# Pooling's neighbour sums moved behind the convolution, and one of two weightings of V moved from VectorE to GpSimd

## The reference

```python
def _pool_mixer(u, w_pool_l, s_pool_l):          # windows 2, 4, 8, 16 over neighbouring tokens
    csum = cumulative sum of u over tokens
    for g, w in enumerate(POOL_WINDOWS):
        mean = (cs[:, hi] - cs[:, lo]) / (hi - lo)
        parts.append(mean - uf[group g])
    y = einsum('btgc,gce->btge', stack(parts), w_pool_l)
    return y * s_pool_l

def _conformer_conv(u, ...):                     # 31 taps, depthwise
    a, g = split(u); h = a * sigmoid(g)
    h = depthwise_conv(h, conv_w_l) + conv_b_l
    return silu(layer_norm(h)) @ w_pw2_l

def _ret_scan(kc, vc, s0):                       # retention, chunks of 128 tokens
    kv = einsum('bhncd,hc,bhnce->nbhde', kc, w_end, vc)
    scan: s -> chunk_decay * s + kv_n            # once forward, once backward
```

## Time and profile before

| | |
|---|---|
| median of 3 runs | 3274.9 us (3274.47 to 3276.96) |
| profiled execution, time | 3276.12 us |
| profiled execution, span from first to last instruction | 3274.0 us |
| PE busy | 2883.8 us, 88% |
| DVE busy | 1996.9 us, 61% |
| ACT busy | 1204.8 us, 37% |
| POOL busy | 608.8 us, 19% |
| mean granted clock of PE | 0.944 of full speed |

### The profile page before, as it was taken

The page is one execution under the profiler, slowest core; times in us unless marked ns, Lnnn a source line. Parts: engine busy times, 40 slices in busy tenths (PEclk is TensorE's granted clock), DMA queues, the critical chain, the costliest instruction groups (busy, mean ns, idle before and its releaser), DMA issues.

```text
span 3274.0 us, 46686 instructions
## 1 busy us (share of the span) xinstructions
PE 2883.8 (88%) x17578; PEld 1603.1 (49%) x17578; DVE 1996.9 (61%) x2744; ACT 1204.8 (37%) x2076; POOL 608.8 (19%) x456
## 2 busy tenths in 40 slices
PE   4799896878999999999997579896789899999997
PEld 3455562554545656757754234463554344444443
DVE  5894687884366414636645695578883664274765
ACT  5111325775444212313324311326773443231332
POOL 0500021000225302202212230011001243120311
PEclk8899996999999999999998789998999999999998
DMA  5111111221134321111141221212222242112133
GB/s 207 55 40 38 36 43 42 89 82 58 60 124 135 121 77 46 49 42 44 48 147 34 96 71 39 49 41 81 101 101 71 93 139 83 45 52 64 52 130 115
DMA packets 69312, 248.90 MB, mean 76 GB/s; under 512 B 9248, under 2 KB 10016, under 8 KB 69152
## 3 DMA queue, kind: packets, MB, share of 16 engines
q1 hardware_dynamic: 68000, 241.44, 22.0%
q10 hardware_dynamic: 1152, 5.24, 0.4%
HBM read 221.75 MB, written 19.92 MB: 74 GB/s over the span
## 4 chain that ended last, share of the span: by engine, by line
PE 61%; issue 18%; DVE 12%; ACT 5%; POOL 2%; DMA 1%; SPq 0%; DVEq 0%; POOLq 0%; ACTq 0%
PE PS L777 36%; PE PS L882 17%; DVE R L2139 4%; DVE wlo L1801 2%; PE PS L1178 2%; ACT X L1430 1%; ACT R L1428 1%; DVE R L1963 1%; DVE R L1950 1%; ACT whi L1313 1%; POOL R L2541 1%; DMA R<-in_w_ada 1%; PE PS L1102 1%; PE PS L1201 1%; PE PS L811 1%
## 5 line engine op out<-in xcount | busy, mean ns | idle before, releaser
L777 PE MATMUL PS<-R,whi 128*128 128x512 f16 (+1 forms) x5216 | 1428.6, 361 | 98.8 <-DVE wlo L1801 57.4
L777 PE MATMUL PS<-R,wlo 128*128 128x512 f16 (+1 forms) x2608 | 940.5, 361 | 0.0
L777 PEld LDWEIGHTS PS<-R,whi 128*128 128x128 f16 x5216 | 509.5, 99 | 633.6 <-issue 72.5
L882 PE MATMUL PS<-R,whi 128*128 128x256 f16 (+2 forms) x2352 | 510.3, 326 | 0.0
L1801 DVE SCALAR_TENSOR_TENSOR wlo<-stage,whi 128x1024 f16<-128x1024 f32 (+1 forms) x204 | 278.6, 1366 | 364.6 <-ACT whi L1313 363.7
L777 PEld LDWEIGHTS PS<-R,wlo 128*128 128x128 f16 x2608 | 257.9, 99 | 256.6 <-issue 14.9
L882 PE MATMUL PS<-R,wlo 128*128 128x256 f16 (+2 forms) x1176 | 319.1, 326 | 0.0
L882 PEld LDWEIGHTS PS<-R,whi 128*128 128x128 f16 x2352 | 230.1, 98 | 152.0
L1313 ACT ACTIVATE whi<-stage 128x1024 f16<-128x1024 f32 (+1 forms) x204 | 210.4, 1031 | 140.4 <-PE PS L777 85.0
L2139 DVE SCALAR_TENSOR_TENSOR R<-X,small,R 128x1024 f32<-128x1024 f32 (+1 forms) x180 | 218.9, 1263 | 1.8
L2468 POOL TENSOR_TENSOR X<-X 128x512 f32<-128x512 f32 (+1 forms) x98 | 135.5, 1386 | 453.7 <-ACT X L1705 331.9
(11 more groups left out here) (219 smaller groups left out, 3468.8 us busy)
## 6 DMA issues: line engine op xcount, KB each, us to landing
stage<-in_w_gu SPq DMA_DIRECT2D x120, 512.0 KB, 3.8
X<-in_w_ada SPq DMA_DIRECT2D x60, 512.0 KB, 3.3
stage<-in_w_down SPq DMA_DIRECT2D x48, 512.0 KB, 3.4
stage<-in_w_in SPq DMA_DIRECT2D x44, 512.0 KB, 3.3
stage<-in_w_out SPq DMA_DIRECT2D x32, 512.0 KB, 3.3
h_save<-R SPq DMA_DIRECT2D x24, 640.0 KB, 5.3
R<-h_save SPq DMA_DIRECT2D x24, 640.0 KB, 4.6
T<-in_w_ada SPq DMA_DIRECT2D x20, 512.0 KB, 3.6
```

What stands on the lines that cost most here:

```text
L777: last = mm(slot(into, t0, t1)[:, c0 - t0:c1 - t0], w[:, j, k, :], row, start=(k == 0 and q == 0), stop=(k == K - 1 and q == 2))
L882: last = mm(s_bank(nf, t, o, n), w[:, j, k0 + k, :], row, start=(k == 0 and x == 0), stop=(k == PAIRS - 1 and x == 2))
```

## The change

Three things change. The pooling sums are started by POOL only when the last tap of the convolution is done (`conv`), and their padded rows and their table lie in the rows `H` in place of `G` and `Y`; so ACT no longer waits for `pooled` ahead of unit 6, but ahead of reading out unit 16, which is written to row `H`. To have the rows `H` free in layer 1, SP saves them to HBM right as the last step of layer 0 finishes each of them, and the tables `cnt` are loaded only behind `u_done` and `h_saved`, in front of the rotary tables. Of the two weightings of V, the forward one goes to POOL, which counts `vw_fwd`.

```diff
-        Gpad = R[:, G:G + 7, :] ... 6 padded rows
+        Gpad = R[:, G:G + 3, :] ... 2 padded rows
+        Hpad = R[:, H:H + 5, :] ... 4 padded rows
...
@@ SP
                 else:
-                    sp.wait_ge(S["h_rows"], rows_before(4 * l + 1, 0))
+                    sp.wait_ge(S["h_back"], 16 * KD * 2 * l)
+                    for d in range(KD):
+                        sp.wait_ge(S["h_rows"], rows_before(4 * l - 1, 1) + d + 1)
+                        sp.dma_start(h_save[d], R[:, H + d, :]).then_inc(S["h_saved"], 16)
                     sp.wait_ge(S["stk_ps"], ...)
-                for j in range(2):
-                    sp.dma_start(R[:, Y + j, :], a["cnt"][j]).then_inc(S["cd_tab"], 16)
                 sp.dma_start(SW[:, :], a["swb"][l]).then_inc(S["cd_tab"], 16)
                 sp.dma_start(perm[:, :], a["permB"]).then_inc(S["cd_tab"], 16)
                 sp.wait_ge(S["u_done"], rows_before(4 * l + 2, 0))
+                if l:
+                    sp.wait_ge(S["h_saved"], 16 * KD * 2 * l)
+                for j in range(2):
+                    sp.dma_start(R[:, H + 5 + j, :], a["cnt"][j]).then_inc(S["cd_tab"], 16)
                 for j in range(2):
                     sp.dma_start(xrow(2 + j), a["ropeB"][j]).then_inc(S["b_tab"], 16)
-                (units 2 to 9, in layer 1 each followed by a save of one row H)
-                stream(unit0(l, "in") + 2 + KD, ahead - 2 - KD, KD, a["w_in"][l][2 + KD:ahead])
+                stream(unit0(l, "in") + 2, ahead - 2, KD, a["w_in"][l][2:ahead])
...
-                if l:
-                    sp.wait_ge(S["h_saved"], 16 * KD * 2 * l)
                 swap(0)
@@ PE
                     pe.wait_ge(S["vw"], at("vw", l) + i + 1)
+                    pe.wait_ge(S["vw_fwd"], at("vw_fwd", l) + i + 1)
@@ ACT
+                if l:
+                    act.wait_ge(S["h_saved"], 16 * KD * 2 * l)      # ahead of unit 0's read-out
-                (units 2 and 3 to Gpad[:, 2, :] and Gpad[:, 3, :])
+                (units 2 and 3 to Hpad[:, 0, :] and Hpad[:, 1, :])
                 act.wait_ge(S["glu"], at("glu", l) + 2)
-                act.wait_ge(S["pooled"], at("pooled", l) + 2)
...
-                if l:
-                    act.wait_ge(S["h_saved"], 16 * KD * 2 * l)
+                act.wait_ge(S["pooled"], at("pooled", l) + 2)
                 a_row(16, 1)
@@ DVE
                     TT(heads(T[:, 512 + c:768 + c]), heads(vtok[:, t, :]), by_head(8, 1), ALU.mult)
-                    TT(heads(vw_fwd[:, c:c + 256]), heads(vtok[:, t, :]), by_head(8, 0), ALU.mult).then_inc(S["vw"], 1)
+                    (the first one now counts vw)
@@ POOL
                 pool.wait_ge(S["cd_tab"], at("cd_tab", l) + 64)
+                pool.wait_ge(S["conv"], at("conv", l) + TAPS * 2 * len(segs(l)))
                 for j in range(2):
                     pool.wait_ge(S["slot_free"], u0 + 3 + j)
-                    src = Gpad[:, 2 + j, :]
-                    a_, b_ = Gpad[:, 4, :], Gpad[:, 5, :]
+                    src = Hpad[:, j, :]
+                    a_, b_ = Hpad[:, 2, :], Hpad[:, 3, :]
...
                 pool.memset(Sb[:, B_ORDER[0], :], 0.0).then_inc(S["states_zero"], 1)
+                pool.wait_ge(S["pw_ps"], at("pw_ps", l) + 2 * len(spans(t0)))
+                for i in range(NTILE):
+                    pool.wait_ge(S["v_tok"], at("v_tok", l) + i + 1)
+                    if i >= 2:
+                        pool.wait_ge(S["kv_ps"], at("kv_ps", l) + i - 1)
+                    TT(heads(vw_fwd[:, (i % 2) * 256:(i % 2) * 256 + 256]), heads(vtok[:, B_ORDER[i], :]), by_head(8, 0),
+                       ALU.mult).then_inc(S["vw_fwd"], 1)
```

More of the change, by code:

```diff
@@ L196, in build @@
         Xpad = X[:, :].rearrange("p (r t) -> p r t", r=4)
-        Gpad = R[:, G:G + 7, :].rearrange("p r t -> p (r t)")[:, 0:6 * PADW].rearrange("p (r t) -> p r t", r=6)
+        Gpad = R[:, G:G + 3, :].rearrange("p r t -> p (r t)")[:, 0:2 * PADW].rearrange("p (r t) -> p r t", r=2)
+        Hpad = R[:, H:H + 5, :].rearrange("p r t -> p (r t)")[:, 0:4 * PADW].rearrange("p (r t) -> p r t", r=4)
         vtok = X[:, 0:NTILE * 256].rearrange("p (t c) -> p t c", c=256)
@@ L245, in build @@
             b_tab=32, gate_tanh=4, roped_ps=12, roped=12, d_tab=16,
-            states_zero=1, tr_ps=NTILE, v_tok=NTILE, k_tok=NTILE, vw=NTILE, kv_ps=NTILE, state=NTILE - 1, kv_fwd=NTILE - 1,
+            states_zero=1, tr_ps=NTILE, v_tok=NTILE, k_tok=NTILE, vw=NTILE, vw_fwd=NTILE, kv_ps=NTILE, state=NTILE - 1, kv_fwd=NTILE - 1,
             state_fwd=NTILE - 1,
@@ L453, in build, with by_head @@
         block = ctx.enter_context(nc.Block())
+        def by_head(col0, half):
+            return rtab[:, col0 + 4 * half:col0 + 4 * half + 4].rearrange("p (h e) -> p h e", e=1).to_broadcast([P, HB, 64])
+        heads = lambda ap: ap.rearrange("p (h e) -> p h e", h=HB)
         B_ORDER = [1, 0] + list(range(NTILE - 1, CT - 1, -1))
@@ L1555, in _ @@
                 u0 = unit0(l, "in")
-                kinds = ((ACT.Tanh, Gpad[:, 0, :]), (ACT.Copy, Xpad[:, 0, :]), (ACT.Copy, Gpad[:, 2, :]),
-                         (ACT.Copy, Gpad[:, 3, :]), (ACT.Tanh, Gpad[:, 1, :]), (ACT.Copy, Xpad[:, 1, :]))
+                if l:
+                    act.wait_ge(S["h_saved"], 16 * KD * 2 * l)
+                kinds = ((ACT.Tanh, Gpad[:, 0, :]), (ACT.Copy, Xpad[:, 0, :]), (ACT.Copy, Hpad[:, 0, :]),
+                         (ACT.Copy, Hpad[:, 1, :]), (ACT.Tanh, Gpad[:, 1, :]), (ACT.Copy, Xpad[:, 1, :]))
                 for i, (kind, dst) in enumerate(kinds):
@@ L2501, in _ @@
                     pool.wait_ge(S["slot_free"], u0)
+                    pool.wait_ge(S["h_saved"], 16 * KD * 2 * l)
                 gaps = [(0, HALF), (HALF + CTX, HALF), (PADW - HALF, HALF)] if not t0 else \
@@ L2504, in _ @@
                 for g0, n in gaps:
-                    pool.memset(Gpad[:, 2:4, g0:g0 + n], 0.0)
+                    pool.memset(Hpad[:, 0:2, g0:g0 + n], 0.0)
                     last = pool.memset(Xpad[:, 0:2, g0:g0 + n], 0.0)
@@ L2522, in _ @@
                             last = TT(R[half:half + 64, Y + 2 + j, c0:c0 + n], w[half:half + 64, p0:p0 + n],
-                                      R[half:half + 64, Y + j, c0:c0 + n], ALU.mult)
+                                      R[half:half + 64, H + 5 + j, c0:c0 + n], ALU.mult)
                     own.link(last)
```

12 lines of the change are left out of this document (1 added, 11 removed).

## The result

| | before | after |
|---|---|---|
| median of 4 runs | 3274.68 us (3273.78 to 3276.96) | 3226.66 us (3223.84 to 3231.61) |
| profiled execution, time | 3276.12 us | 3231.61 us |
| profiled execution, span | 3274.0 us | 3229.8 us |
| PE busy | 2883.8 us | 2881.9 us |
| DVE busy | 1996.9 us | 1973.3 us |

The ratio of the times is 0.9855, with a 95% interval from 0.9842 to 0.9867: 48 us faster.

The account below looks back on a forecast made before the run. PE, 88% busy, was taken as the bound. 25.0 + 20.6 + 6.2 - 3.0 - 1.1 = 47.7 us off 3276.1 gives 3228.4, put at 3227 us against the runs' median; 8 in 10 range 3218 to 3246.

Parts of the forecast that it names:

- taps, layer 0: Convolution taps no longer beside POOL's sums, so PE never stalls and unit 7 ends at 173.7 us; gain 25.0 us.
- taps, layer 1: Same in layer 1: taps at undisturbed length, units up to 7 end at 1933.9 us, before 1954.6; gain 20.6 us.
- V's weighting, both layers: Retention's state loop: DVE loses the forward product, 0.34 us for each of nine chunks; gain 3.1 us a layer, 6.2 in all.
- contention, layer 1: Moved sums lengthen DVE's instructions in the rotary units, stalling PE at units 13 and 14; cost 3.0 us, at most 10.7.
- contention, layer 0: Moved sums beside layer 0's rotary units, where a unit with its rotary products takes 14.3 us; cost 0, at most 5.
- table DMAs: Two table rows ahead of unit 2's weights: hidden in layer 0, unit 2 late in layer 1; cost 1.1 us, bounds 0 and 3.
- rival 2: State loop: POOL's product comes first, DVE waits, chunks take 2.5 us, not 1.65; 16 us, total 3243 us; chance 0.11.
- five exposed instructions: Rotary units: five DVE instructions per unit with both inputs in SBUF, slowed beside POOL's sums to 2.75 us each.
- 11.6 of PE plus what slack is left: Layer 1, unit 14: PE's time set against DVE's about 17 us, leaving a stall of 1.6 us.
- the rule: Shared ports held for each instruction's whole duration: layer 1 stall about 6 us, total 3 us higher.
- the rows gave 3.0: Layer 1 rotary units: cost from the profiled pitch of taps beside POOL's sums, 3.3 us, taken as 2.75 for rotary instructions.
- twice the costs: Contention and DMA costs doubled, given as the slow end, 3236 us, of the forecast's own range from 3219.

Follow-up runs that it names:

- experiment 3: Changed kernel without POOL's wait for the convolution's last tap, so the sums start beside the first taps as before; 3271.0 us.
- the next two profiles: Profiles of two repeat runs of the changed kernel, nothing altered; medians 3227.36 and 3227.57 us.
- experiment 4: Changed kernel with the pooling sums left out, one fill with zeros per row in their place; 3225.14 us.
- experiment 7: Changed kernel with four waits among POOL's twelve sums of layer 1, so they run where DVE is idle; 3224.51 us.
- Experiments 6 and 8: Weights of units 2 and 3 requested ahead of the table rows: on the changed kernel with lo formed earlier, 3227.9 us; on it with paced sums, 3220.3 us.
- the second run of the changed kernel: The changed kernel run again with nothing altered; median 3227.36 us, span of its profile 3226.0 us.

## Why the prediction was right, step by step

It said 3227 us; the median is 3226.7. By terms, gains positive:

| term | predicted | the stages show |
|---|---|---|
| taps, layer 0 | +25.0 | 102.93 - 77.88 = +25.05 |
| taps, layer 1 | +20.6 | 88.05 - 68.12 + 0.72 = +20.65 |
| V's weighting, both layers | +6.2 | 2 x 2.4 = +4.8 |
| contention, layer 1 | -3.0 | 1.6 + 2.4 = -4.0 |
| contention, layer 0 | 0 | 0 |
| table DMAs | -1.1 | -0.7 (0.5 to 0.9) |
| sum | 47.7 | 45.8 |

**The taps** came out to a tenth in both layers. The step that did it was to follow PE's units and DVE's list side by side with the lengths of an undisturbed stretch. Apart from unit 2's 0.7 us in layer 1, PE had no hole between units 1 and 10, as foretold, and experiment 3 shows that the sums' time, not their rows, was the cause.

**V's weighting** was sized too large. The instruction saved is worth 0.33 to 0.34 us a chunk (1.99 to 1.66), as predicted, but I counted nine chunks. From the first product to the last there are eight steps, and the first of them gained next to nothing, 1.97 us: there DVE and POOL did meet. That leaves seven, 2.4 us a layer. They also meet ahead of the first product, which the loop's time leaves out: it comes 1.00 us after DVE begins to weight V (2062.19 to 2063.19), before 0.82 (2103.35 to 2104.17). So rival 2, POOL in DVE's way, was real at the head of each loop and cost 0.3 us inside it and 0.2 ahead of it. POOL's product took 0.61 to 0.62 us once the loop ran, not the 0.88 of the earlier trace rows: one ends at 2072.50, when DVE's next one starts (2072.49). In the first profile layer 0 showed 0.5 us only, which would have been a wrong lesson: PE's lower clock hid most of the rest, and the next two profiles show 2.4. What the medians give for this part beyond 4.8 us is not settled.

**Contention** was sized too small. For unit 13 the working held: I had put five exposed instructions at 2.75 us, 13.8 us from the rotary part's start to the end of `lo_part`, and they took 13.9 (1959.15 to 1973.01). PE waits 1.45 us for it, predicted 1.3. Unit 14 is the mis-sized one, 2.4 us where 1.6 were predicted. DVE's side of it was right: about 17 us from the end of unit 12's products to the end of `lo_part`, and 17.3 measured (1970.17 to 1987.51). What the prediction set against them, "11.6 of PE plus what slack is left", it did not work out, and it was 0.8 us too much. PE is also held in the rotary products ahead of both units, 0.2 and 0.3 us, which the sum did not have. That these stalls are the sums' is shown by experiment 4 (left out, the 4.0 us go) and experiment 7 (moved into DVE's gaps, they go as well). As cost they count for less: in both experiments 0.6 us come back before the state loop, at PE's lower clock.

By the Trainium skill (SBUF — State Buffer, the section on the two separate sides), an instruction of DVE with two SBUF inputs and one of POOL hold a shared pair of ports each for its whole length. The trace agrees in which instructions suffer: L2175, L2176 and L1805 do, and those that read PSUM do not (0.69 and 1.21 us). On the price it lies between: the rule gave about 6 us of stall in layer 1, the rows gave 3.0, and 4.0 were measured.

**The table DMAs** cost 0.7 us for 1.1 predicted; in layer 0 they are hidden, as said (`whi` of unit 2 at 90.77 us, unit 1 read at 95.60). Experiments 6 and 8 remove the delay by order alone.

The terms' errors, 1.4 too much gain and 0.6 too little loss, make the sum 1.9 us too large against the stages. The difference of the medians is 48.0 all the same. In the profile of the second run of the changed kernel, 48.0 us below before, the stages above hold 45.5 us and the other 2.5 lie in stretches that the change does not touch or touches lightly: 0.6 ahead of unit 1, 1.1 between the two layers' loops and units, 0.8 between unit 16 and the loop of layer 1, and 0.4 less 0.3 elsewhere. The 0.8 are a matter of PE's clock: the 16 products ahead of that loop take 9.78 us before and 8.83 there. The hit to within half a microsecond is thus partly luck; the 46 us of the stages are not. One sum of the prediction is wrong and bears on nothing else: twice the costs are 4.1 us more and would end the forecast's own range at 3231 us, not 3236.

## What to carry to other kernels

When one engine's instructions are suddenly two or three times as long, look for the other engine's run with the same first and last microsecond, and move that run before tuning either. Where there is no free place, split it: a few waits on a semaphore that the loaded engine already counts let the other work in its gaps, whereas a new order on the loaded engine moves the wait and may lengthen it. And read a small gain in a second profile before it is called absent.

## What the runs showed of the hardware

- Two engines that contend do not share evenly: in layer 1 of after DVE's 0.42 us instruction became 2.45 to 2.76 and its 1.22 us one 3.30, while POOL's 2.39 us ones took 2.39 to 3.33. The short instruction pays for the long one's length.
- Four products of 128 columns in f32 took 1.06 us at a granted clock of 0.52 and 0.60 at 1.00. The same stretch of the same kernel was at 0.52 in one execution and at 1.00 in the next two. In the 7 us before it, counted from the same instruction, PE was busy for 5.03 us at the full clock in all three. The only difference found ahead of it is small: the 4 us before those 7 had a granted clock of 0.91 in the one and of 0.96 and 0.95 in the others, so PE had come back from the low level a little later.
- Taking a stall away can cost some of it again further on: with 4.0 us of stall gone, the clock fell earlier in a later wait of PE, and 16 products took 9.46 us in place of 8.83. The same products took 8.79 us in experiment 3, which has none of those stalls, so a shorter way there does not always bring the lower clock.
